# Expert result rows: copied by GpSimd and stored from GpSimd's queue in place of ScalarE's

## The chip, the cores and the metric
One core of one Trainium2 chip runs the whole program. The metric is the device time of one execution in microseconds, as the median of several runs. The five engines are TensorE (PE), VectorE (DVE), ScalarE (ACT), GpSimd (POOL) and SyncE (SP).

## What is computed
One hybrid block (dilated attention beside gated linear attention), a mixture of 32 experts with 4 chosen for each of 512 tokens, and a second block (pooling and an RWKV-style recurrence). The change lies in the mixture of experts:

```python
def expert_block(args):
    idx, e = args
    xb = xpad[idx]
    gu = xb @ w_gate_up[e] + b_gate_up[e]
    x_glu = jnp.minimum(gu[:, ::2], SWIGLU_LIMIT)
    x_lin = jnp.clip(gu[:, 1::2], -SWIGLU_LIMIT, SWIGLU_LIMIT)
    act = x_glu * jax.nn.sigmoid(SWIGLU_ALPHA * x_glu) * (x_lin + 1.0)
    return act @ w_down[e] + b_down[e]

out_buf = lax.map(expert_block, (tok_buf.reshape(n_blocks, MOE_BLOCK), blk_e))
out = jnp.zeros((T + 1, D), out_buf.dtype).at[tok_buf].add(out_buf)
```

The model's width is 1024, the experts' inner width 1024, all numbers are float32. `b_down` and the gates are applied in the stage after the experts.

## The kernel before
The program runs in stages. In `stage_experts` the tokens of each expert are cut into units of 32 rows; a unit's 32 x 1024 rows lie on 128 partitions as four quarters of 256 columns. The number of units is known only at run time (each engine loads it into a register, `units_on`), and each engine runs a loop over them, `Fori(1, units)`. The engines meet only through semaphores.

*SyncE* loads the weights, 32 experts of 12 chunks of 1 MB (8 of gate and up, 4 of down), into 18 slots of `staging`. A chunk's slot is free when the last unit of the expert that lay there has used it (`free`), and at most five loads are under way (L1657 issues, L1641 counts the arrival of the chunk four before).

*VectorE and ScalarE* copy three quarters of each chunk from `staging` to one of four places of `ring` (L1865, L1788): positions 0, 1, 3, 4, 6, 8, 9, 11 of a unit by VectorE, 2, 5, 7, 10 by ScalarE. The first quarter is read from `staging` directly.

*TensorE* does in each turn of its loop: `up(i)`, eight chunks of four column groups (L1730); `down(i - 1)`, four chunks (L1753), into bank 4; `turn_hidden(i)` (L1739); `turn_rows(i + 2)` (L1707); the bias of the next unit (L1717). `down` starts only once `y_read` says that bank 4 was read.

*ScalarE*'s turn: the fills of positions 5, 7 and 10, `gate`, `rows_turned`, the fill of position 2 of the next unit, then `read_y(i - 1)` (L1811), which copies the result of the unit before from bank 4 to `y_rows`, `store_y(i - 1)` (L1816), which issues its store to `expert_rows` in HBM, and `hidden_turned(i)` (L1799), which `down(i)` needs. `read_y` waits for `y_out`: the store before must have landed, as there is one `y_rows`.

```python
def read_y(n, done):
    act.wait_ge(chunk_done, done)
    act.wait_ge(y_out, 16 * n + 16)
    act.activation(y[:], k.bank(4)[:, 0:GLU], ACT.Copy).then_inc(y_read, 1)

def store_y(n):
    act.wait_ge(y_read, n + 1)
    act.sem_inc(y_seen, 1)
    act.dma_start(store_of(n * SLOTS), y[:]).then_inc(y_out, 16)
```

*GpSimd*'s turn: `move_rows(i + 2)` (L1681) waits for the gather of those rows and for `turn_rows` of the unit before them, and copies `rows_landing` to `rows`; `gather(i + 3)` loads the unit's code, copies its indices to `slot` (L1670) and issues the indirect DMA of its rows (L1673).

Of the kernel before, what the change touches and what calls it, by code (L numbers as in the profile page):

```python
# [21 lines left out]
P = 128  # L22
S = 512
NT = S // P
D = 1024
# [7 lines left out]
NE, TOPK = 32, 4  # L33
SLOTS = 32
QUARTERS = 4
EXTRA = (S * TOPK) // (SLOTS + 1)
NBLK = NE + EXTRA
# [4 lines left out]
TABLE = ENDS + NE + LINE  # L42
# [1493 lines left out]
def stage_experts(k):  # L1536

    nc, d = k.nc, k.d
    with ExitStack() as ctx:
        sb = lambda n, s, dt=F32: k.sb(n, s, dt, at=ctx)  # L1540
        sem = k.stage_semaphores(ctx)
# [6 lines left out]
        landing = sb("rows_landing", [P, D // QUARTERS])  # L1548
# [3 lines left out]
        glu = sb("glu", [P, GLU])  # L1552
        hT = sb("hiddenT", [P, 2, P])
        y = sb("y_rows", [P, D // QUARTERS])
        gsum = sb("gsum", [P, LINE])
        raw_bias = ring[:, RING - 1, 0:PART]
        hidden = glu
# [10 lines left out]
        rows_in = sem("rows_in")  # L1568
# [13 lines left out]
        turned_ps = sem("hidden_turned_ps")  # L1582
        hT_ready = sem("hiddenT_ready")
        y_read = sem("expert_y_read")
        y_seen = sem("expert_y_seen")
        y_out = sem("expert_y_out")
        settled = sem("early_settled")
# [3 lines left out]
        def units_on(eng):  # L1591
            return eng.value_load(k.table[0:1, TABLE - 1:TABLE], min_val=NE, max_val=NBLK)

        def expert_on(eng, i):
            return eng.value_load(k.table[0:1, bass.ds(i, 1)], min_val=0, max_val=NE - 1)

        def after(eng, sem, n):

            if not isinstance(n, int) or n > 0:
                eng.wait_ge(sem, n)  # L1600
# [21 lines left out]
        def store_of(n):  # L1622
            return d["expert_rows"][bass.ds(n, SLOTS), :].rearrange("r (c n) -> c r n", c=QUARTERS)

        with nc.Block() as block:
# [37 lines left out]
            @block.gpsimd  # L1663
            def _(pool):
                units = units_on(pool)
                by_quarter = d["h2"].rearrange("t (c n) -> (t c) n", c=QUARTERS)

                def gather(i, out, at, done):
                    code = pool.value_load(k.table[0:1, bass.ds(i + P, 1)], min_val=0, max_val=CODES - 1)
                    pool.tensor_copy(slot[:, at:at + 1], k.slots[:, bass.ds(code, 1)]).then_inc(slot_ready, 1)  # L1670
                    pool.wait_ge(slot_ready, i + 1)
                    pool.sem_inc(slot_seen, 1)
                    pool.indirect_dma_start(  # L1673
                        out=out[:], out_offset=None, in_=by_quarter,
                        in_offset=bass.IndirectOffsetOnAxis(ap=slot[:, at:at + 1], axis=0)).then_inc(done, 16)

                def move_rows(i):
                    pool.wait_ge(rows_in, 16 * i - 16)
                    pool.wait_ge(rows_ps, i)
                    pool.sem_inc(rows_free, 1)  # L1680
                    pool.tensor_copy(rows[:], landing[:]).then_inc(rows_here, 1)  # L1681
                    pool.wait_ge(rows_here, i + 1)
                    pool.sem_inc(rows_moved, 1)

                gather(0, y, 1, first_in[0])
                gather(1, rows, 2, first_in[1])
                gather(2, landing, 0, rows_in)
                for m in range(2):
                    pool.wait_ge(first_in[m], 16)
                    pool.sem_inc(rows_here, 1)  # L1690
                move_rows(2)
                gather(3, landing, 0, rows_in)
                with pool.Fori(1, units) as i:
                    move_rows(i + 2)
                    gather(i + 3, landing, 0, rows_in)
                pool.wait_ge(rows_in, 16 * units + 16)

            @block.tensor
            def _(pe):
# [82 lines left out]
            def _(act):  # L1782
                units = units_on(act)

                def fill(i, e, pos):
                    act.wait_ge(chunk_in, e * CHUNKS + (pos + 1))
                    after(act, chunk_done, i * CHUNKS + (pos - RING + 1))
                    act.activation(ring[:, pos % RING, :], staged(i, e, pos, PART, CHUNK - PART), ACT.Copy  # L1788
                                   ).then_inc(act_filled, 1)

                def gate(i):
                    act.wait_ge(lin_ready, i + 1)
                    after(act, turned_ps, i)
                    act.activation(glu[:], k.bank(0)[:, 0:GLU], ACT.Silu, scale=ALPHA).then_inc(glu_ready, 1)

                def hidden_turned(i):
                    act.wait_ge(turned_ps, i + 1)
                    act.wait_ge(chunk_done, i * CHUNKS + CHUNKS)
                    act.activation(hT[:].rearrange("p b n -> p (b n)"), k.bank(2)[:, 0:2 * P], ACT.Copy,  # L1799
                                   scale=1.0 / ALPHA).then_inc(hT_ready, 1)  # L1800

                def rows_turned(i, done):
                    act.wait_ge(rows_ps, i + 1)
                    after(act, chunk_done, done)
                    act.activation(rowsT[:].rearrange("p b n -> p (b n)"), k.bank(6)[:, 0:2 * P], ACT.Copy
                                   ).then_inc(rowsT_ready, 1)

                def read_y(n, done):
                    act.wait_ge(chunk_done, done)
                    act.wait_ge(y_out, 16 * n + 16)  # L1810
                    act.activation(y[:], k.bank(4)[:, 0:GLU], ACT.Copy).then_inc(y_read, 1)  # L1811

                def store_y(n):
                    act.wait_ge(y_read, n + 1)
                    act.sem_inc(y_seen, 1)
                    act.dma_start(store_of(n * SLOTS), y[:]).then_inc(y_out, 16)  # L1816

                act.sem_inc(y_out, 16)
                rows_turned(0, 0)
                fill(0, 0, 2)  # L1820
                act.wait_ge(bias_set, 1)
# [13 lines left out]
                with act.Fori(1, units) as i:  # L1835
                    e = expert_on(act, i)
                    fill(i, e, 5)
                    fill(i, e, 7)
                    fill(i, expert_on(act, i - 1), 10)
                    gate(i)  # L1840
                    rows_turned(i + 1, i * CHUNKS + KT)
                    fill(i + 1, expert_on(act, i + 1), 2)
                    read_y(i - 1, i * CHUNKS + CHUNKS)
                    store_y(i - 1)
                    hidden_turned(i)
                act.wait_ge(act_filled, units * len(BY_ACT) + 1)
                act.sem_inc(act_filled, 2)
# [2 lines left out]
                act.activation(k.gates[:], k.gates[:], ACT.Exp).then_inc(gate_exp, 1)  # L1850
                end = act.value_load(k.table[0:1, TABLE - 2:TABLE - 1], min_val=NE - 1, max_val=NBLK - 1)
                read_y(end, units * CHUNKS + CHUNKS)
                store_y(end)
                act.wait_ge(y_out, 16 * units + 16)
                act.sem_inc(y_seen, 1)

            @block.vector
            def _(dve):
# [1273 lines left out]
```

## Time and profile before

| | |
|---|---|
| median of 3 runs | 1996.08 us (1993.56 to 2001.99) |
| the profiled execution | 1999.55 us |
| its span, first to last instruction | 1997.8 us |
| TensorE's granted clock, mean | 0.929 |
| busy: PE / DVE / ACT / POOL | 85% / 57% / 43% / 16% |
| moved by DMA | 516.46 MB, mean 259 GB/s |
| weights of the experts' stage | 250 + 128 loads of 1 MB by SyncE, 6 early ones |
| stores of result rows | 80 of 128 KB on ScalarE's queue (q10) |
| gathers of rows | 83 of 128 KB on GpSimd's queue (q0) |

How to read it: busy shares are means over stages with different limits, and a matmul's group counts time in which others run beside it. What bounds a stage is read from the waits in that stretch. "Landing" is the time at which a DMA's completion was counted.

### The profile page before, as it was taken

Reading aid. Unit: us, or ns where it says so; the run is one execution under the profiler, and the core shown is the slowest. Engines: PE = TensorE matmul, PEld = TensorE weight load, DVE = VectorE, ACT = ScalarE, POOL = GpSimd, SP = SyncE. Lnnn points to the kernel's source line nnn. Section 1 sums busy time; section 2 is a strip of 40 time slices with the busy share of each in tenths; the row PEclk is TensorE's granted clock in tenths of the full one; section 3 lists DMA queues with packets and bytes.
Section 4 is the critical chain, followed back from the end, with each engine's and each line's share of the span. In section 5 each row is a group of like instructions: output and inputs, shape, how many; then the busy total and the mean of one; then the engine's idle time right before and its main releaser. Section 6 shows DMA issues by size and latency. Waiting matters only on the chain. (4 is left out here: it accounts for less than half of the span.)

```text
span 1997.8 us, 50227 instructions
## 1 busy us (share of the span) xinstructions
PE 1695.5 (85%) x16925; PEld 877.7 (44%) x16926; DVE 1139.1 (57%) x1698; ACT 859.4 (43%) x1131; POOL 326.4 (16%) x307
## 2 busy tenths in 40 slices
PE   6999888698898899888887789878887658998797
PEld 3999645232233333333332233333232226777763
DVE  5874535574566566555654456556554454784555
ACT  5334522254455455444543445445443334433411
POOL 0000000121222222222221122222111030260000
PEclk9999988798999999999998899999888778999999
DMA  8870850539669888992699986996898872221011
GB/s 315 281 264 11 230 206 35 239 151 425 264 273 423 366 338 338 425 401 105 260 424 404 400 336 278 424 374 279 346 426 331 341 260 69 79 74 45 6 53 42
DMA packets 134386, 516.46 MB, mean 259 GB/s; under 512 B 11411, under 2 KB 60324, under 8 KB 85029
## 3 DMA queue, kind: packets, MB, share of 16 engines
q1 hardware_dynamic: 116884, 483.61, 61.4%
q0 software_dynamic: 6720, 20.85, 2.8%
q10 hardware_dynamic: 10706, 10.96, 1.7%
q8 instruction: 51, 0.84, 0.2%
q14 instruction: 25, 0.20, 0.0%
HBM read 492.57 MB, written 22.81 MB: 258 GB/s over the span
## 5 line engine op out<-in xcount | busy, mean ns | idle before, releaser
L1865 DVE COPY ring<-staging 128x1536 f32 (+1 forms) x638 | 602.9, 961 | 428.9 <-PE banks L1730 285.7
L1730 PE MATMUL banks<-staging,rowsT 128*32 (+1 forms) x1268 | 650.1, 654 | 185.0 <-ACT ring L1788 149.8
L1730 PE MATMUL banks<-ring,rowsT 128*32 128x512 f32 x3840 | 661.1, 656 | 0.0
L1788 ACT ACTIVATE ring<-staging 128x1536 f32 (+1 forms) x319 | 465.3, 1481 | 400.3 <-PE banks L1730 145.4
L1730 PEld LDWEIGHTS banks<-staging,rowsT 128*32 128x32 f32 x1268 | 128.8, 115 | 630.3 <-issue 625.4
L1753 PE MATMUL banks<-staging,hiddenT 128*32 x1280 | 297.6, 387 | 2.3 <-ACT hiddenT L1799 2.1
L1753 PE MATMUL banks<-ring,hiddenT 128*32 128x256 f32 x3840 | 298.5, 386 | 0.0
L1753 PEld LDWEIGHTS banks<-staging,hiddenT 128*32 128x32 f32 x1280 | 141.9, 113 | 163.5 <-issue 71.2
L1681 POOL COPY rows<-rows_landing 128x256 f32<-128x256 f32 x80 | 74.8, 935 | 794.9 <-PE banks L1707 794.9
L1753 PEld LDWEIGHTS banks<-ring,hiddenT 128*32 128x32 f32 x3840 | 156.9, 113 | 0.0
L602 PE MATMUL banks<-w_in_hi,hT 128*128 128x256 f32 (+1 forms) x768 | 147.0, 291 | 1.1 <-issue 1.1
L1730 PEld LDWEIGHTS banks<-ring,rowsT 128*32 128x32 f32 x3840 | 144.9, 115 | 0.0
L1673 POOL DMA_INDIRECT rows_landing<-h_rows,slot x81 | 133.4, 1647 | 64.3 <-POOL slot L1670 64.3
L2208 PE MATMUL banks<-h3T,w_in_hi 128*128 128x512 f32 x400 | 128.9, 404 | 1.4 <-DVE h3T L2386 1.4
L602 PEld LDWEIGHTS banks<-w_in_hi,hT 128*128 128x128 f32 x768 | 122.2, 193 | 3.1 <-issue 3.0
L602 PE MATMUL banks<-w_in_lo,hT 128*128 128x256 f32 (+1 forms) x384 | 109.5, 285 | 0.0
L1670 POOL COPY slot<-slots 128x1 int32 x83 | 49.4, 595 | 276.0 <-issue 206.2
L1874 DVE TENSOR_SCALAR lin<-banks 128x256 f32<-128x256 f32 x80 | 34.0, 425 | 96.3 <-PE banks L1730 96.3
L2208 PEld LDWEIGHTS banks<-h3T,w_in_hi 128*128 128x128 f32 x400 | 75.6, 190 | 22.9 <-issue 4.1
L1799 ACT ACTIVATE hiddenT<-banks 128x256 f32<-128x256 f32 x80 | 30.7, 384 | 113.0 <-PE banks L1730 98.7
L2208 PE MATMUL banks<-h3T,w_in_lo 128*128 128x512 f32 x200 | 78.5, 392 | 0.0
L1811 ACT ACTIVATE y_rows<-banks 128x256 f32<-128x256 f32 x80 | 30.0, 375 | 108.3 <-DMA expert_rows<-y_rows 97.5
(435 smaller groups left out, 1949.7 us busy)
## 6 DMA issues: line engine op xcount, KB each, us to landing
staging<-in_w_gate_up SPq DMA_DIRECT2D x250, 1024.0 KB, 13.3
staging<-in_w_down SPq DMA_DIRECT2D x128, 1024.0 KB, 13.3
stage<-in_w_mod SPq DMA_DIRECT2D x21, 1024.0 KB, 5.4
stage<-in_w_in SPq DMA_DIRECT2D x25, 512.0 KB, 4.0
stage<-in_w_in SPq DMA_DIRECT2D x11, 1024.0 KB, 6.7
expert_rows<-y_rows ACTq DMA_DIRECT2D x80, 128.0 KB
expert_rows<-catT SPq DMA_DIRECT2D x1, 7936.0 KB
early<-in_w_gate_up SPq DMA_DIRECT2D x6, 1024.0 KB, 13.5
```

The lines of the kernel that those rows point to most:

```text
L602: mm = pe.matmul(k.bank(4 + t)[:, 0:w], hT[:, a, q, tt], b[:, q, :], start=(q == 0 and a == 0 and b is hi), stop=(q == KT - 1 and a == 1))
L1670: pool.tensor_copy(slot[:, at:at + 1], k.slots[:, bass.ds(code, 1)]).then_inc(slot_ready, 1)
L1673: pool.indirect_dma_start(out=out[:], out_offset=None, in_=by_quarter, in_offset=bass.IndirectOffsetOnAxis(ap=slot[:, at:at + 1], axis=0)) ...
L1681: pool.tensor_copy(rows[:], landing[:]).then_inc(rows_here, 1)
L1730: mm = pe.matmul(k.bank(0)[c * SLOTS:(c + 1) * SLOTS, :], rowsT[:, q % 2, row], w, start=first and q == 0, stop=not first and q == KT - 1, ...
L1753: mm = pe.matmul(k.bank(4)[c * SLOTS:(c + 1) * SLOTS, 0:GLU], hT[:, b, m * SLOTS:(m + 1) * SLOTS], w, start=(m == 0 and b == 0), stop=(m = ...
L1788: act.activation(ring[:, pos % RING, :], staged(i, e, pos, PART, CHUNK - PART), ACT.Copy).then_inc(act_filled, 1)
L1799: act.activation(hT[:].rearrange("p b n -> p (b n)"), k.bank(2)[:, 0:2 * P], ACT.Copy, scale=1.0 / ALPHA).then_inc(hT_ready, 1)
L1811: act.activation(y[:], k.bank(4)[:, 0:GLU], ACT.Copy).then_inc(y_read, 1)
L1865: dve.tensor_copy(ring[:, pos % RING, :], staged(i, e, pos, PART, CHUNK - PART)).then_inc(dve_filled, 1)
L1874: dve.tensor_scalar(lin[:], k.bank(0)[:, GLU:PART], LIMIT + 1.0, 1.0 - LIMIT, ALU.min, ALU.max).then_inc(lin_ready, 1)
L2208: mm = pe.matmul(k.bank(n % 4), w[:, n % NW, q, :], hT[:, b, q, :], start=(q == 0 and a == 0), stop=(q == KT - 1 and a == 2))
```

## The change
A new buffer `rows_leaving` takes the place of `y_rows` as the source of the store. GpSimd copies `y_rows` to it, waits for its own copy, and issues the store from its own queue, at the end of each turn of its loop; the turn of unit 1 now stands ahead of the loop. ScalarE's `read_y` waits for `y_free` (GpSimd has copied the rows before) in place of `y_out` (they have landed), and issues no store. GpSimd's copy waits for `y_read`, and for `y_out` of the store before.

```diff
+        leaving = sb("rows_leaving", [P, D // QUARTERS])
...
+                def store_rows(n):
+                    pool.wait_ge(y_read, n + 1)
+                    after(pool, y_out, 16 * n)
+                    pool.sem_inc(y_due, 1)
+                    pool.tensor_copy(leaving[:], y[:]).then_inc(y_free, 1)
+                    pool.wait_ge(y_free, n + 2)
+                    pool.sem_inc(y_seen, 1)
+                    pool.dma_start(store_of(n * SLOTS), leaving[:]).then_inc(y_out, 16)
...
-                with pool.Fori(1, units) as i:
+                pool.sem_inc(y_free, 1)
+                move_rows(3)
+                gather(4, landing, 0, rows_in)
+                store_rows(0)
+                with pool.Fori(2, units) as i:
                     move_rows(i + 2)
                     gather(i + 3, landing, 0, rows_in)
+                    store_rows(i - 1)
+                end = pool.value_load(k.table[0:1, TABLE - 2:TABLE - 1], min_val=NE - 1, max_val=NBLK - 1)
+                store_rows(end)
                 pool.wait_ge(rows_in, 16 * units + 16)
+                pool.wait_ge(y_out, 16 * units)
+                pool.sem_inc(y_seen, 1)
...
                 def read_y(n, done):
                     act.wait_ge(chunk_done, done)
-                    act.wait_ge(y_out, 16 * n + 16)
+                    act.wait_ge(y_free, n + 1)
                     act.activation(y[:], k.bank(4)[:, 0:GLU], ACT.Copy).then_inc(y_read, 1)
 
-                def store_y(n):
-                    act.wait_ge(y_read, n + 1)
-                    act.sem_inc(y_seen, 1)
-                    act.dma_start(store_of(n * SLOTS), y[:]).then_inc(y_out, 16)
-
-                act.sem_inc(y_out, 16)
...
                     read_y(i - 1, i * CHUNKS + CHUNKS)
-                    store_y(i - 1)
                     hidden_turned(i)
...
                 read_y(end, units * CHUNKS + CHUNKS)
-                store_y(end)
-                act.wait_ge(y_out, 16 * units + 16)
-                act.sem_inc(y_seen, 1)
```

On ScalarE, at the end of its turn of the experts' loop, the order before is this:

```order
L1788 ACTIVATE ring<-staging 128x1536
L1809 REGISTER_ALU
L1810 ISA
L1811 ACTIVATE y_rows<-banks 128x256
L1816 ISA
L1816 DMA expert_rows<-y_rows 4x32x256
L1799 ACTIVATE hiddenT<-banks 128x256
```

and after the change this:

```order
L1809 ACTIVATE ring<-staging 128x1536
L1830 REGISTER_ALU
L1832 ACTIVATE y_rows<-banks 128x256
L1820 ACTIVATE hiddenT<-banks 128x256
L1850 REGISTER_ALU
L1850 COMPARE_AND_BRANCH
```

The store is gone from between the copy of the result rows and `hiddenT`.

On GpSimd, the whole turn of its loop before:

```order
L1681 COPY rows<-rows_landing 128x256
L1682 REGISTER_ALU
L1669 ISA
L1669 TENSOR_LOAD table
L1669 ISA x2
L1670 ISA
L1670 COPY slot<-slots 128x1
L1671 REGISTER_ALU
L1673 DMA rows_landing<-h_rows,slot 128x256
L1693 REGISTER_ALU
L1693 COMPARE_AND_BRANCH
```

and the second half of the turn after the change:

```order
L1673 COPY slot<-slots 128x1
L1674 REGISTER_ALU
L1676 DMA rows_landing<-h_rows,slot 128x256
L1603 ISA
L1692 COPY rows_leaving<-y_rows 128x256
L1693 REGISTER_ALU
L1695 ISA
L1695 DMA expert_rows<-rows_leaving 4x32x256
L1709 REGISTER_ALU
L1709 COMPARE_AND_BRANCH
```

The copy to `rows_leaving` and the store stand behind the gather, and ahead of the next turn's move of rows. TensorE's, VectorE's and SyncE's instructions keep their order.

## Rows read from the trace of the kernel before

**Rows 1.** Timeline of TensorE, turning the hidden rows: start us, us, instruction.
```profile
897.99 0.44 PE L1739 MATMUL banks<-sq,glu 128*128 128x128 f32 x2
...
911.64 0.44 PE L1739 MATMUL banks<-sq,glu 128*128 128x128 f32 x2
...
929.36 0.44 PE L1739 MATMUL banks<-sq,glu 128*128 128x128 f32 x2
...
941.26 0.44 PE L1739 MATMUL banks<-sq,glu 128*128 128x128 f32 x2
```

**Rows 2.** The tile `y_rows`: its durations min/median/max in ns, first and last start.
```profile
L1811 ACT ACTIVATE y_rows<-banks x80: 360/383/390, 409.9 to 1596.3; 128x256 f32<-128x256 f32 x80
```

**Rows 3.** TensorE's waits from 410 to 1600: total us, times, longest us.
```profile
PE banks L1730 <- ACT ring L1788: 149.8, 92, 4.7
```

**Rows 4.** ScalarE's waits, the same stretch.
```profile
ACT y_rows L1811 <- DMA expert_rows<-y_rows: 97.5, 36, 4.5
```

**Rows 5.** Timeline of ScalarE, two units in a loaded stretch; idle time in brackets.
```profile
900.60 0.39 ACT L1811 ACTIVATE y_rows<-banks 128x256 f32<-128x256 f32 x1 [1.63 <-DMA expert_rows<-y_rows]
901.25 1.07 ACTq L1816 DMA_DIRECT2D expert_rows<-y_rows  x1
...
916.62 0.38 ACT L1811 ACTIVATE y_rows<-banks 128x256 f32<-128x256 f32 x1 [4.01 <-DMA expert_rows<-y_rows]
...
918.43 0.38 ACT L1799 ACTIVATE hiddenT<-banks 128x256 f32<-128x256 f32 x1 [1.42 <-issue]
919.87 2.86 ACT L1788 ACTIVATE ring<-staging 128x1536 f32 x2 [1.06 <-issue]
```

**Rows 6.** Timeline of ScalarE where the DMA engines have little to do.
```profile
942.77 1.05 ACTq L1816 DMA_DIRECT2D expert_rows<-y_rows  x1
...
954.06 0.36 ACT L1811 ACTIVATE y_rows<-banks 128x256 f32<-128x256 f32 x1
```

**Rows 7.** DMA queues from 654 to 669: packets, MB, share of 16 engines.
```profile
q1 hardware_dynamic: 845, 6.14, 96.8%
q10 hardware_dynamic: 132, 0.13, 2.5%
q0 software_dynamic: 48, 0.13, 2.2%
```

**Rows 8.** Timeline of GpSimd, one turn.
```profile
912.47 1.11 POOL L1681 COPY rows<-rows_landing 128x256 f32<-128x256 f32 x1 [8.59 <-PE banks L1707]
...
915.80 1.72 POOL L1673 DMA_INDIRECT rows_landing<-h_rows,slot  x1 [0.79 <-POOL slot L1670]
```

**Rows 9.** Lines L1673, L1681 and L1865: durations min/median/max in ns; a landing.
```profile
L1673 POOL DMA_INDIRECT rows_landing<-h_rows,slot x81: 966/1722/1726, 375.0 to 1559.7; - x81
...
DMA to landing us min/median/max: 6.2/6.2/6.2
...
L1681 POOL COPY rows<-rows_landing x80: 397/1091/1152, 384.9 to 1557.5; 128x256 f32<-128x256 f32 x80
...
L1865 DVE COPY ring<-staging x638: 945/960/1187, 386.9 to 1591.2; 128x1536 f32 x158, 128x1536 f32<-128x1536 f32 x2
```

**Rows 10.** Windows: length, PE, PEld, DVE, ACT, POOL busy, PEclk, DMA share, GB/s.
```profile
457.00:515.00 58.00, 44.42 (x405) 13.76 (x402) 26.88 (x35) 21.65 (x25) 7.54 (x9) 0.82 1.01 425
636.00:667.00 31.00, 25.49 (x277) 9.88 (x270) 17.28 (x23) 14.65 (x17) 6.77 (x6) 0.94 1.01 426
929.00:989.00 60.00, 59.05 (x679) 23.42 (x672) 42.34 (x56) 35.61 (x41) 16.92 (x15) 1.00 0.40 155
```

**Rows 11.** ScalarE's waits for the store from 636:698, 819:912, 1007:1055 and 1256:1350.
```profile
ACT y_rows L1811 <- DMA expert_rows<-y_rows: 10.7, 4, 4.1
...
ACT y_rows L1811 <- DMA expert_rows<-y_rows: 14.8, 6, 3.7
...
ACT y_rows L1811 <- DMA expert_rows<-y_rows: 7.6, 3, 3.6
...
ACT y_rows L1811 <- DMA expert_rows<-y_rows: 13.0, 5, 3.7
```

**Rows 12.** Timeline behind the last unit.
```profile
1601.83 0.94 POOL L2323 DMA_INDIRECT mixer<-expert_rows,dest  x1 [41.13 <-POOLq L192]
```

More of the change, by code:

```diff
@@ L1584, in stage_experts @@
         y_read = sem("expert_y_read")
+        y_due = sem("expert_y_due")
+        y_free = sem("expert_y_free")
         y_seen = sem("expert_y_seen")
```

## The prediction, made before the changed kernel ran

> **What bounds the kernel now.** I read the views in this order: the waits of each engine in the expert stage, the timeline of single units, the windows with the DMA share, and the queues. A unit is one pass of 32 rows through one expert; there are 80 of them. The reference's routing, worked out on its inputs, gives the 32 experts these units in order: 5, 1, 2, 5, 3, 2, 2, 3, 3, 3, 2, 2, 2, 7, 2, 2, 1, 2, 2, 3, 4, 2, 2, 2, 3, 4, 1, 2, 3, 1, 1, 1.
>
> The reader should first see what a unit costs when nothing holds it up. TensorE turns the hidden rows once a unit, and two such rows are 941.26 - 929.36 = 11.9 us apart [rows 1]. At that pace 80 units are 952 us. ScalarE's 80 copies of the result rows start from 409.9 to 1596.3 us [rows 2], 79 steps in 1186 us, where 79 x 11.9 would be 940: about 246 us are lost. TensorE's idle time there ends mostly on ScalarE's fills of the ring: 149.8 us in 92 waits [rows 3]. Why is ScalarE late? It waited 97.5 us, in 36 of the 80 units, for the store of the last result rows to land before it could overwrite `y_rows` [rows 4].
>
> The timeline shows how that reaches TensorE. The store issued at 901.25 lets the next copy start only at 916.62, so the round trip is 15.4 us; the copy stood 4.01 us, then came the issue, then `hiddenT` at 918.43, and only at 919.87 the fills that TensorE needs [rows 5]. The two units from 897.99 to 929.36 take 13.65 and 17.72 us, 31.4 in place of 23.8 [rows 1]. That is 7.6 us lost for 1.63 + 4.01 = 5.6 us of waiting: each microsecond of this wait costs TensorE about 1.35. Where the DMA engines have little to do, the wait isn't there: the store issued at 942.77 is no hindrance at 954.06 [rows 6].
>
> Why 15 us for 128 KB? In 15 us of a loaded stretch ScalarE's queue q10 moved 132 packets for 0.13 MB: 128 rows of 1 KB and four small ones, so I read it as four engines with 32 rows each. The weights' queue q1 had 845 packets and 96.8% of 16 engines, about 0.27 us a packet (0.968 x 16 x 15 / 845) [rows 7]. If an engine takes one packet from each queue in turn, 32 rows wait behind 32 weight packets, some 10 us, and issue and completion make up the rest.
>
> **The change, part by part.**
> *Removed on ScalarE: the wait for the landing.* Upper bound of what it gives: 97.5 x 1.35 = 132 us. *Removed on ScalarE: the issue.* From the start of the copy to `hiddenT` are now 1.8 us, about 1.4 of them after the copy has ended [rows 5]. In a unit without the wait TensorE doesn't wait for ScalarE at all (11.9 us), so this gives nothing more there; in the others it lies in the 1.35. I cost it at 0; the cover is TensorE's own work.
>
> *Added on GpSimd: copy, wait, issue.* Its unit today runs from 912.47 to 917.52, 5.1 us, of which the copy of rows is 1.11 and the wait between the slot's copy and the gather 0.79 [rows 8]. The new copy has the same shape (128x256 f32): 1.1 us. A wait on its own copy: 0.8. The issue: the gather's takes 0.97 to 1.73 us [rows 9]; I take 1.7. Together 3.6, so that GpSimd is occupied 8.7, with the loop's registers about 9 us of 11.9. Queued behind the new wait for `y_read` are the next move of rows and the next gather: both start about 4 us later in their unit than now. The moved rows are needed one unit later, 11.9 us after the point at which the move may start, and are ready after about 4 + 1.1; cover 6 us. The gather is issued about 9 us into the unit and lands 6.2 us after its issue [rows 9], while the next move begins at 11.9 + 4; that just fits, with a cover of under 1 us ahead of the 6 us of the rows themselves. Cost: 0. If the cover went, `turn_rows` on TensorE would wait.
>
> *The new round trip.* ScalarE now waits for GpSimd's copy of the rows before, and that copy for the landing of the store before it. GpSimd's queue q0 moved a gather of the same 128 KB as 48 packets, 32 of 4 KB and 16 small ones [rows 7]: two data packets an engine in place of 32 rows. If the store is cut like this, its round trip is the 6.2 us of the gather, plus copy 1.1 and wait 0.8: a period of 8.1 us, under 11.9. The bounds, since no row shows a store on this queue: 6.2 at the low end, and at the high end today's 32 rows an engine, 15.4 with 0.65 us more for the issue. I take the low one, because both transfers have rows of 1 KB on both sides. The Trainium skill ("DMA: Bandwidth & Descriptors", "Queues, rings and completion order") says that the slowest dimension of the access pattern picks how many engines share a transfer, for both kinds of queue. The four engines of q10 agree with that, as the store's pattern is 4x32x256. By it the new store would also sit on four engines; with 4 KB packets that is 8 an engine, about 6 x 0.45 us more, a period of 10.8 us, still under 11.9, and the sum stays.
>
> The copy and the issue could also be slowed by VectorE. GpSimd's copies take 397 ns to 1152 ns, nearly always the long value, while VectorE's 638 fills stay between 945 and 1187 [rows 9]: GpSimd is the one that gives way, and 1.1 and 1.7 already contain it. VectorE: 0. The Trainium skill ("SBUF — State Buffer", "SBUF: two separate sides") has a rule against this change: while VectorE copies f32 within SBUF, GpSimd can't write the descriptors of its DMAs, and an issue of 620 ns takes about 3100. The trace agrees in direction, not in size: 1.73 is the longest gather. With 3.1 for each of its two DMAs GpSimd would be occupied 11.8 us a unit, just at the pace, and nothing would be left to spare.
>
> *What the weights take back.* In the two units 636 to 667 the DMA share is 1.01 at 426 GB/s [rows 10]: an expert's 12.6 MB with the rows of two units can't come in less than 30.8 us, and two units want 23.8. So a two-unit expert gains only as far as weights are there ahead: 18 slots less 12 are half an expert, 15.4 us at most. The waits in the two-unit runs are 10.7 + 14.8 + 7.6 + 13.0 = 46.1 of the 97.5 us [rows 11]. Lower end: no lead, all of that comes back as waits for weights, and 51.4 x 1.35 = 69 us are saved. Upper end: full lead; then only the two runs of three such experts overdraw it, by 3 x 7.0 - 15.4 = 5.6 each, and 132 - 11 = 121 are saved. The one lone and one two-unit expert from 457 to 515 should need 60.9 us of stream and took 58, so that hardly 3 us of lead was there, although five units stood before them [rows 10]. But the experts of three units and more leave 4.9 us and more each for the stream to get ahead, and from 929 to 989, in the expert of seven, its share is 0.40: there it had run out of free slots. Between the two I take the middle, 95.
>
> *The four engines relieved.* The store's packets are 2.5% of 16 engines over 15 us, 6.0 us of work, 1.5 on each of four [rows 7]. If weight loads waited for these, up to 1.2 us a loaded unit would come free. A share of 1.01 over all sixteen says that the others weren't idle meanwhile; I take 0 and let it widen the low end.
>
> *The end.* The last copy starts at 1596.3 and the gathers of the next stage at 1601.83 [rows 12]; the copy and the wait on GpSimd put 1 us to 2 us in. Cost 1.
>
> Sum: 1999.55 - 95 + 1 = 1905.6 for the profiled execution, which stands 3.5 us above the median of the runs. **Forecast 1902 us.**
>
> **The rivals.**
> *A. The weights take back more.* Each two-unit expert stays at 30.8 us. For it: share 1.01, and 457 to 515. Against it: 929 to 989 has a share of 0.40 [rows 10], so after long experts all slots must be full. Time: 1996 - 69 + 1 = 1928; with some of the other units' gain lost as well, up to 1960.
> *B. Slower: the store's round trip on GpSimd's queue becomes the pace.* If GpSimd sends the rows one by one on four engines, the trip is 16.0 us, and copy and wait make the period 17.9, against 16.0 between the copies at 900.60 and 916.62. It decides from 11.9 us on (gain shrinks) and makes the kernel slower above 16. In the 36 units that wait today that is 36 x 1.9 = 68 us: 2064. Against it: the 48 packets of the gather.
> *C. Nothing changes.* The fills come late for TensorE's own reasons (ScalarE's fills wait for TensorE too) and the stage is held by the weights throughout. Against it: 929 to 989, and the timeline. Or GpSimd's period comes out near 15. Time 1996, from 1986 to 2006.
>
> **How the numbers follow.** A measurement of this kernel can tell about 0.5%, 10 us, from no change. The forecast's own case, 1876 to 1928, has 0.64; A 0.20, B 0.10, C 0.06. Faster 0.84, same 0.06, slower 0.10. The range leaves out B and C, and takes in A to 1960; below, 1865, for the four engines. That leaves out 0.16 and the tails.
>
> **What would show it.** The wait of `y_rows` for the DMA must be gone from ScalarE's waits, and nothing of size for GpSimd in its place. TensorE's waits for ScalarE's fills fall from 149.8 us to about half, and those for VectorE's fills, 32 us now, rise, as waiting for weights shows there. The DMA share in 800 to 1500 rises. Units in the loaded stretches come at 11.9 us, with single long ones behind two-unit runs. q0 has 48 packets more a unit. GpSimd's idle time before the copy of rows, now nearly all of its time, stays above 2 us a unit. Wrong would be: ScalarE's copy waits for GpSimd's, GpSimd's copy for a DMA of over 10 us, or `turn_rows` on TensorE for `rows`.

## The result and the profile after

The changed kernel takes 1901.84 us (median of 4 runs, 1900.64 to 1903.0) against 1998.28 us (4 runs): a ratio of 0.952, 95% interval 0.9495 to 0.9542. The forecast was 1902. The profiled execution took 1903.0 us with a span of 1901.4, 96.4 less than before. The total is right to the microsecond; the terms it was summed from are not, as the rest shows, so that this closeness is luck.

| from the traces, us | before | after | difference |
|---|---|---|---|
| first to last copy of result rows, 79 steps | 1186.4 | 1083.2 | -103.2 |
| TensorE's wait into the next stage | 5.8 | 10.8 | +5.0 |
| all else in the span | 805.6 | 807.4 | +1.8 |
| span | 1997.8 | 1901.4 | -96.4 |

**Waits.** ScalarE's waits of the changed kernel from 410 to 1600 (total us, times, longest) have one line on the result rows, in place of [rows 4]:

```profile
ACT y_rows L1832 <- PE banks L1774: 1.0, 1, 1.0
```

The 97.5 us are gone. They haven't moved to GpSimd: of its waits up to 1495 the largest is for new result rows, and the landing of a store held it up four times.

```profile
POOL rows_leaving L1692 <- ACT y_rows L1832: 606.5, 76, 24.4
...
POOL rows_leaving L1692 <- DMA expert_rows<-rows_leaving: 16.7, 4, 5.3
```

TensorE's waits, against [rows 3]:

```profile
PE banks L1751 <- ACT ring L1809: 67.4, 40, 3.1
PE banks L1751 <- DVE ring L1876: 42.2, 39, 4.4
...
PE banks L2169 <- DVE z L2456: 10.8, 1, 10.8
```

Those for ScalarE's fills fell from 149.8 to 67.4 us, those for VectorE's rose from 32.2 to 42.2: what is left comes mostly with the arrival of weights. The last line is the wait into the next stage.

**The unit.** Here is ScalarE's timeline of one unit, at the place that [rows 5] and [rows 6] show of before:

```profile
902.93 0.36 ACT L1832 ACTIVATE y_rows<-banks 128x256 f32<-128x256 f32 x1
903.19 0.38 ACT L1820 ACTIVATE hiddenT<-banks 128x256 f32<-128x256 f32 x1
905.31 1.49 ACT L1809 ACTIVATE ring<-staging 128x1536 f32 x1 [1.74 <-PE banks L1751]
...
914.44 0.36 ACT L1832 ACTIVATE y_rows<-banks 128x256 f32<-128x256 f32 x1
```

A unit now takes 914.44 - 902.93 = 11.5 us, where [rows 1] had 11.9 as the pace of an undisturbed one. 53 of the 79 steps run at 11.5, where 20 ran at 11.9 before. That was not forecast. The granted clock is 1.00 at both places, so it isn't the clock. `hiddenT` follows the copy by 0.26 us in place of 1.8, and the fills wait for TensorE instead of the other way round.

**GpSimd.** The first two rows below are the tiles' durations (min/median/max in ns), the others its timeline of one turn.

```profile
L1692 POOL COPY rows_leaving<-y_rows x80: 393/410/1107, 409.6 to 1494.2; 128x256 f32<-128x256 f32 x80
...
L1695 POOL DMA_DIRECT2D expert_rows<-rows_leaving x80: 713/874/1542, 410.8 to 1495.3; - x80
...
607.32 0.42 POOL L1692 COPY rows_leaving<-y_rows 128x256 f32<-128x256 f32 x1 [5.18 <-ACT y_rows L1832]
608.53 0.87 POOL L1695 DMA_DIRECT2D expert_rows<-rows_leaving  x1 [0.78 <-POOL rows_leaving L1692]
609.39 0.41 POOL L1684 COPY rows<-rows_landing 128x256 f32<-128x256 f32 x1
...
611.72 1.12 POOL L1676 DMA_INDIRECT rows_landing<-h_rows,slot  x1 [0.81 <-POOL slot L1673]
```

The turn is 607.32 to 612.84, 5.5 us, where 8.7 were forecast. Both copies take 0.41 us in place of 1.1. They now start as a fill of VectorE ends or just before, and run mostly in the gaps in which VectorE waits for TensorE (607.50 to 608.17 and 609.49 to 609.89 here).

**The DMA engines.** The packets of the page, before and then after:

```profile
DMA packets 134386, 516.46 MB, mean 259 GB/s; under 512 B 11411, under 2 KB 60324, under 8 KB 85029
```
```profile
DMA packets 135347, 516.60 MB, mean 272 GB/s; under 512 B 20051, under 2 KB 58724, under 8 KB 85989
...
q0 software_dynamic: 18240, 31.46, 4.6%
```

q0 had 6720 packets before, so each of the 80 stores is 11520 / 80 = 144 packets. The small ones rose by 8640 = 80 x 108; with the four that ScalarE's store had, that is 112 a store, and 32 packets are left for its 128 KB, 4 KB each. The last store goes out alone, so the order of its packets can be read: these are all DMA packets first from 1496.0 to 1497.6, then from 1497.6 to 1500.0.

```profile
DMA packets 112, 0.02 MB, mean 11 GB/s; under 512 B 108, under 2 KB 108, under 8 KB 112
```
```profile
DMA packets 32, 0.11 MB, mean 48 GB/s; under 512 B 4, under 2 KB 4, under 8 KB 32
```

Of the 112 small packets 108 come first, with four of the 4 KB ones, and only four come with the other 28. By size the 112 are 96 of 16 bytes and 16 of 4 bytes, and 4 bytes is also the size of ScalarE's four small ones. I read the 16 as completions: twelve of engines that carry no data, and four of engines that carry all of it, eight packets of 4 KB each. So on GpSimd's queue too four engines carry the store; what differs from ScalarE's is that the rows go four to a packet. Over the stage (410 to 1596, and 410 to 1490) the DMA share rose:

```profile
410.00:1596.00 1186.00, 1001.64 (x10517) 372.87 (x10516) 663.43 (x869) 558.71 (x630) 250.50 (x234) 0.92 0.83 341
```
```profile
410.00:1490.00 1080.00, 968.09 (x10480) 371.50 (x10476) 666.05 (x862) 550.22 (x626) 261.33 (x392) 0.94 0.91 375
```

**The end of the stage.** GpSimd's timeline there, against [rows 12]:

```profile
1494.19 0.40 POOL L1692 COPY rows_leaving<-y_rows 128x256 f32<-128x256 f32 x1 [3.60 <-DMA expert_rows<-rows_leaving]
1495.35 0.71 POOL L1695 DMA_DIRECT2D expert_rows<-rows_leaving  x1 [0.76 <-POOL rows_leaving L1692]
1502.82 1.02 POOL L2334 DMA_INDIRECT mixer<-expert_rows,dest  x1 [6.76 <-POOLq L192]
```

From the last copy of ScalarE (1492.2) to the next stage's first gather it is 10.6 us, where it was 5.5 before: the last copy of GpSimd waits for the landing of the store before it, then come a wait, an issue and a landing.

### The profile page after: what moved, and what is told of

Read it like the earlier page. It is cut to its first block and busy times, and to the rows that moved or that the text cites. A ratio compares the mean times of both kernels' runs of the same rounds, so it can differ in the third digit from the quotient of the medians.

```text
span 1901.4 us, 50539 instructions
## 1 busy us (share of the span) xinstructions
PE 1665.0 (88%) x16925; PEld 878.1 (46%) x16926; DVE 1144.6 (60%) x1698; ACT 852.6 (45%) x1131; POOL 338.2 (18%) x467
## 5 line engine op out<-in xcount | busy, mean ns | idle before, releaser
L1809 ACT ACTIVATE ring<-staging 128x1536 f32 (+1 forms) x319 | 472.1, 1485 | 526.6 <-PE banks L1751 260.5
L1751 PE MATMUL banks<-staging,rowsT 128*32 (+1 forms) x1268 | 607.1, 622 | 112.7 <-ACT ring L1809 67.4
L1751 PE MATMUL banks<-ring,rowsT 128*32 128x512 f32 x3840 | 617.6, 624 | 0.0
L1774 PE MATMUL banks<-staging,hiddenT 128*32 x1280 | 308.4, 397 | 2.0 <-ACT hiddenT L1820 0.5
L1774 PE MATMUL banks<-ring,hiddenT 128*32 128x256 f32 x3840 | 309.5, 397 | 0.0
L1692 POOL COPY rows_leaving<-y_rows 128x256 f32<-128x256 f32 x80 | 34.5, 431 | 623.2 <-ACT y_rows L1832 606.5
L1676 POOL DMA_INDIRECT rows_landing<-h_rows,slot x81 | 108.8, 1343 | 65.9 <-POOL slot L1673 65.9
L1695 POOL DMA_DIRECT2D expert_rows<-rows_leaving x80 | 71.3, 891 | 66.7 <-POOL rows_leaving L1692 60.6
L602 PEld LDWEIGHTS banks<-w_in_lo,hT 128*128 128x128 f32 x384 | 74.2, 193 | 1.9 <-issue 1.9
L1673 POOL COPY slot<-slots 128x1 int32 x83 | 23.2, 279 | 285.8 <-issue 235.2
## 6 DMA issues: line engine op xcount, KB each, us to landing
staging<-in_w_gate_up SPq DMA_DIRECT2D x250, 1024.0 KB, 12.6
```

The lines of the kernel that those rows point to most:

```text
L602: mm = pe.matmul(k.bank(4 + t)[:, 0:w], hT[:, a, q, tt], b[:, q, :], start=(q == 0 and a == 0 and b is hi), stop=(q == KT - 1 and a == 1))
L1676: pool.indirect_dma_start(out=out[:], out_offset=None, in_=by_quarter, in_offset=bass.IndirectOffsetOnAxis(ap=slot[:, at:at + 1], axis=0)) ...
L1692: pool.tensor_copy(leaving[:], y[:]).then_inc(y_free, 1)
L1695: pool.dma_start(store_of(n * SLOTS), leaving[:]).then_inc(y_out, 16)
L1751: mm = pe.matmul(k.bank(0)[c * SLOTS:(c + 1) * SLOTS, :], rowsT[:, q % 2, row], w, start=first and q == 0, stop=not first and q == KT - 1, ...
L1774: mm = pe.matmul(k.bank(4)[c * SLOTS:(c + 1) * SLOTS, 0:GLU], hT[:, b, m * SLOTS:(m + 1) * SLOTS], w, start=(m == 0 and b == 0), stop=(m = ...
```

## The experiments

Three theories stood against each other. *The trip*: the old store's round trip of 15 us is the cause, and this comes from its access pattern. *The buffer*: `rows_leaving` decouples ScalarE from the landing. *The issue*: what counts is that ScalarE no longer issues. The kernel before ran again beside every group.

### e1: the copy stays, ScalarE issues the store

```diff
 def store_rows(n):
     ...
     pool.tensor_copy(leaving[:], y[:]).then_inc(y_free, 1)
-    pool.wait_ge(y_free, n + 2)
-    pool.sem_inc(y_seen, 1)
-    pool.dma_start(store_of(n * SLOTS), leaving[:]).then_inc(y_out, 16)
...
     hidden_turned(i)
+    act.wait_ge(y_free, n + 2)
+    act.sem_inc(y_seen, 1)
+    act.dma_start(store_of(n * SLOTS), leaving[:]).then_inc(y_out, 16)
```

> The changed kernel, but ScalarE issues the store of rows_leaving, behind hiddenT. Theory 1 (the trip of the store is what counted: ScalarE's queue puts 32 rows on each of four engines, issue to landing 14.3 us in a loaded stretch; on GpSimd's queue it is 7 to 7.7): GpSimd's copy must still wait for the landing, ScalarE for the copy, so the period stays at 15 to 16 us in loaded stretches and the time at 1980 to 2010 us, with 90 us or more of waits that begin with the DMA. Theory 2 (the second buffer decouples ScalarE from the landing): 1900 to 1920 us. Theory 3 (the issue on ScalarE is what counted): about half of the gain is gone, 1930 to 1960, and no wait for a DMA.

Measured: 2028.58 us, ratio 1.014 (1.0102 to 1.0175). It is slower than the kernel before, and by more than the theory of the trip had it. GpSimd's waits, and ScalarE's timeline around two stores:

```profile
POOL rows_leaving L1692 <- DMA expert_rows<-rows_leaving: 463.8, 41, 12.4
```
```profile
899.79 1.05 ACTq L1834 DMA_DIRECT2D expert_rows<-rows_leaving  x1
...
911.23 0.38 ACT L1817 ACTIVATE hiddenT<-banks 128x256 f32<-128x256 f32 x1
915.65 1.08 ACTq L1834 DMA_DIRECT2D expert_rows<-rows_leaving  x1
918.17 2.86 ACT L1806 ACTIVATE ring<-staging 128x1536 f32 x2 [6.57 <-issue]
```

Two issues are 15.9 us apart, as before the change. The buffer alone gives nothing: as long as one store at a time is in flight and takes 15 us, its pace is everyone's. ScalarE now waits for GpSimd's copy, which waits for the landing, and the fills stand behind that; even an undisturbed unit takes 12.5 us (27 of the 79 steps). The theory of the buffer falls, for one store in flight; two in flight were not tried.

### e2: GpSimd stores `y_rows` itself, no copy, no second buffer

```diff
 def store_rows(n):
+    pool.wait_ge(y_out, 16 * n)       # not for unit 0
+    pool.sem_inc(y_free, 1)
     pool.wait_ge(y_read, n + 1)
-    after(pool, y_out, 16 * n)
-    pool.sem_inc(y_due, 1)
-    pool.tensor_copy(leaving[:], y[:]).then_inc(y_free, 1)
-    pool.wait_ge(y_free, n + 2)
     pool.sem_inc(y_seen, 1)
-    pool.dma_start(store_of(n * SLOTS), leaving[:]).then_inc(y_out, 16)
+    pool.dma_start(store_of(n * SLOTS), y[:]).then_inc(y_out, 16)
```

> The changed kernel without rows_leaving and without the copy: GpSimd stores y_rows itself, and tells ScalarE of the landing once its own gather is issued. Theory 1: a trip of 7 to 8 us ends before the next result rows are due at 11.5 us, so the copy and the buffer weren't needed: 1895 to 1910 us, waits of y_rows under 15 us in sum. Theory 2: ScalarE again waits for a landing, so the old waits come back: 1970 us or more.

Measured: 1902.73 us, ratio 0.9515 (0.9487 to 0.9543), no different from the changed kernel. The tile `y_rows` (its store's issue in ns, and its time to landing in us):

```profile
L1693 POOL DMA_DIRECT2D expert_rows<-y_rows x80: 712/1546/1565, 409.1 to 1497.8; - x80
...
DMA to landing us min/median/max: 3.9/9.1/10.6
```

9.1 us, and at most 10.6, lie under the 11.5 of a unit. So the copy that the change adds isn't needed.

### e3: the old store with another slowest dimension

The store writes its 128 partitions to one contiguous stretch. The rows then stand in another order in HBM and the next stage gathers other values; the work is the same.

```diff
 def store_of(n):
-    return d["expert_rows"][bass.ds(n, SLOTS), :].rearrange("r (c n) -> c r n", c=QUARTERS)
+    return d["expert_rows"][bass.ds(n, SLOTS), :].rearrange("r (c n) -> (r c) n", c=QUARTERS)
```

> The kernel before, but the store writes the 128 partitions to one contiguous stretch of expert_rows, so that its slowest dimension is 128 and not 4; the same bytes in another order, so the rows that the next stage gathers hold other values. Buffer, wait and issue on ScalarE stay. Theory 1: the trip falls from 14.3 us to 6 to 9, ScalarE's wait for it from 97.5 us to under 15; units at full pace keep 11.9 us since ScalarE still issues: 1905 to 1935 us. Theories 2 and 3: nothing that counts was changed, 1985 to 2005 us.

Measured: 1889.58 us, ratio 0.9446 (0.9417 to 0.9474). With the buffer, the wait and the issuing engine of before, this one line gives more than the whole change. The tile `y_rows`, and the page's packets:

```profile
L1816 ACTq DMA_DIRECT2D expert_rows<-y_rows x80: 347/349/398, 410.5 to 1487.8; - x80
...
DMA to landing us min/median/max: 1.7/6.8/7.7
```
```profile
DMA packets 135346, 516.46 MB, mean 273 GB/s; under 512 B 12371, under 2 KB 61284, under 8 KB 85989
```

The store lands after 6.8 us in the median, and its issue takes 349 ns in place of 1072. There are 960 packets more than before, all of the small kind: 12 a store, so 16 in place of 4. That fits one completion for each engine that takes part, sixteen and four, and the theory of the trip. It went below the forecast of 1905 to 1935 because the pace fell to 11.5 too. The 12 us under the changed kernel are 5.9 in the 79 steps (1077.3) and 6.6 in TensorE's wait into the next stage, which is 4.2 here and 10.8 there.

### e4 and e7: what the issue costs

Why 11.5 and not 11.9? In e4 ScalarE also issues a small load in each turn:

```diff
     read_y(i - 1, i * CHUNKS + CHUNKS)
+    small_dma(i - 1)                  # d["token"], 128 partitions of 20 bytes
     hidden_turned(i)
```

> The changed kernel, plus one small load (128 partitions of 20 bytes) that ScalarE issues between the copy of the result rows and hiddenT, where the store's issue stood. It tests the pace of a unit alone: 11.9 us before, 11.5 after. If the issue on ScalarE makes its fill of position 5 late by 0.4 us in every unit: the pace is 11.9 again, TensorE shows a gap of about 0.4 us in the middle of the eight chunks, and the time rises by 8 to 28 us, to 1910 to 1930. If the pace has another cause (the four engines of the store, the longer turn of GpSimd): 11.5 stays, and 1900 to 1905 us.

Measured: 1906.31 us, ratio 0.9536 (0.9507 to 0.9565); the pace stayed at 11.5. The load's issue took 0.34 us and came ahead of the copy, where ScalarE has time, so that it answered only for a short issue. The time lies between the two forecasts, 4.5 us above the changed kernel, and no run shows why. In e7 the added DMA is a small store with the old pattern, behind a wait for the copy, and nobody waits for it to land:

```diff
+    act.wait_ge(y_read, n + 1)
+    act.sem_inc(small_due, 1)
+    act.dma_start(d["small"][bass.ds(n * SLOTS, SLOTS), :].rearrange("r (c n) -> c r n", c=QUARTERS),
+                  k.sq[:, ONES, 0:8]).then_inc(small_out, 16)
```

> The changed kernel, plus a store of 128 pieces of 32 bytes in the old pattern (4x32x8) that ScalarE issues between the result rows and hiddenT; nobody waits for its landing. The issue of this pattern takes 1.05 to 1.07 us, where the small load took 0.34 and the contiguous store 0.35. If this issue made the unit 11.9 us long in place of 11.5: pace 11.9, a gap of 0.4 us ahead of chunk 5, 1906 to 1925 us. If not, 11.5 and under 1906.

Measured: 1919.55 us, ratio 0.9588 (0.9561 to 0.9615), 17.7 above the changed kernel. Its ScalarE:

```profile
890.07 0.36 ACT L1834 ACTIVATE y_rows<-banks 128x256 f32<-128x256 f32 x1
890.69 1.08 ACTq L1839 DMA_DIRECT2D small_rows<-sq  x1
891.87 0.38 ACT L1822 ACTIVATE hiddenT<-banks 128x256 f32<-128x256 f32 x1 [1.44 <-PE banks L1753]
893.31 2.86 ACT L1811 ACTIVATE ring<-staging 128x1536 f32 x2 [1.05 <-PE banks L1753]
...
901.98 0.37 ACT L1834 ACTIVATE y_rows<-banks 128x256 f32<-128x256 f32 x1
```

The same intervals as before the change, and the pace is 11.9 again. The two fills of positions 5 and 7 stand back to back behind it, and the fill of position 5 is what TensorE misses by 0.4 us: its matmuls at 894.13 and 894.93 are 0.80 us apart, the others 0.43. So an issue of 1.07 us between the copy and `hiddenT` costs 0.4 us a unit even where no one waits for a landing.

### e5: two buffers, and the last store from ScalarE

```diff
-    pool.tensor_copy(leaving[:], y[:]).then_inc(y_free, 1)
-    pool.wait_ge(y_free, n + 2)
-    pool.sem_inc(y_seen, 1)
-    pool.dma_start(store_of(n * SLOTS), leaving[:]).then_inc(y_out, 16)
+    pool.sem_inc(y_free, 1)
+    pool.dma_start(store_of(n * SLOTS), y_of(n)).then_inc(y_out, 16)   # half n % 2 of y_rows
...
     read_y(end, units * CHUNKS + CHUNKS)
+    act.wait_ge(y_read, end + 1)
+    act.sem_inc(y_last_due, 1)
+    act.dma_start(store_of(end * SLOTS), y_of(end)).then_inc(y_last, 16)
```

> The changed kernel without the copy: ScalarE writes to two halves of y_rows in turn, GpSimd stores each straight from there, one store in flight, and the last unit's store is issued by ScalarE itself without waiting for the one before. It tests the end of the stage, where the changed kernel lost 5 us (TensorE's wait for the next stage is 10.8 us long, 5.8 before), since the last copy waits 3.6 us for a landing and is followed by a wait and a slower landing. If these are the cause, 4 to 6 us come back: 1896 to 1898 us. If the loss comes from the next stage's own work: 1901 to 1903.

Measured: 1900.38 us, ratio 0.9494 (0.9468 to 0.952). TensorE's wait into the next stage:

```profile
PE banks L2177 <- DVE z L2464: 6.2, 1, 6.2
```

The wait is down from 10.8 to 6.2, so the 5 us at the end do come from the last store. But the time fell by 1.5 only: the 79 steps took 1087.3 us against 1083.2. Why these 4 us were lost is open; GpSimd's issue has a median of 1247 ns there, against 874. (e2, also without the copy, has 1546 ns and 1088.6 us.)

### e6 and e11: a complete result on sixteen engines

e6 is the kernel before with four stores of 32 partitions a unit, all from ScalarE:

```diff
-    act.dma_start(store_of(n * SLOTS), y[:]).then_inc(y_out, 16)
+    for c in range(QUARTERS):
+        act.dma_start(d["expert_rows"][bass.ds(n * SLOTS, SLOTS), c * GLU:(c + 1) * GLU],
+                      y[c * SLOTS:(c + 1) * SLOTS, :]).then_inc(y_out, 16)
```

> The kernel before, but each unit's rows go out as four stores of 32 partitions each from ScalarE, so that the slowest dimension is 32 and sixteen engines share each; the result is complete and in order, the buffer and the wait for the landing are those of before. Theory 1 (the four engines are the whole cause): four issues of 0.35 us in place of one of 1.07, a landing after 7 to 9 us, no wait for it, 1888 to 1905 us. If the queue rather than the pattern were the cause: 1990 us or more.

Measured: 1926.2 us, ratio 0.962 (0.9593 to 0.9648). The wait for the landing is gone, as the theory of the trip wants, but the forecast was missed by 21 us: the four issues take 1.77 us together, and all stands at 12.4 us a unit.

```profile
904.24 0.36 ACT L1811 ACTIVATE y_rows<-banks 128x256 f32<-128x256 f32 x1
904.85 1.77 ACTq L1817 DMA_DIRECT2D expert_rows<-y_rows  x4
906.71 0.38 ACT L1799 ACTIVATE hiddenT<-banks 128x256 f32<-128x256 f32 x1 [2.12 <-PE banks L1730]
```

e11 issues the same four stores one turn later, behind the fill of position 7:

```diff
     fill(i, e, 7)
+    store_y(i - 2)                    # from turn 2 on; turn 1 stands ahead of the loop
     ...
     read_y(i - 1, i * CHUNKS + CHUNKS)
-    store_y(i - 1)
     hidden_turned(i)
```

> The kernel before, with four stores of 32 partitions each, issued by ScalarE not between the result rows and hiddenT but one turn later, behind its fill of position 7. If the 12.4 us a unit of the run with four stores (issues of 1.77 us ahead of the next fill) is the late fill of position 5: the pace is 11.5 to 11.6 again, and the time 1886 to 1900 us, as with the contiguous store. The landing must come within about 8 us of the issue, else ScalarE waits for it and the pace stays at 12 or more, 1915 to 1930.

Measured: 1894.66 us, ratio 0.9488 (0.9464 to 0.9513), and 1081.5 us for the 79 steps. There is no single pace: 21 steps lie between 11.3 and 11.8 us, 39 others between 10.6 and 13.5. The waits for the landing have become short, but they are there in 43 units; the line below is from 400 to 1490:

```profile
ACT y_rows L1811 <- DMA expert_rows<-y_rows: 25.7, 43, 1.5
```

Of the kernels with a complete result this has the lowest median, 7 us under the changed one (1893.08 to 1900.7 against 1900.64 to 1903.0, measured in different groups; the intervals of the two ratios overlap, so that the order isn't settled), without GpSimd and without a second buffer.

### e8, e9, e10: what holds the stage now

In e8 half of each weight chunk is left out from the 37th on:

```diff
+    whole = CHUNK if m < 2 * STAGED else CHUNK // 2
     sp.dma_start(staging[:, m % STAGED * CHUNK:m % STAGED * CHUNK + whole],
                  (up(e, c) if c < KT else down(e, c - KT))[:, 0:whole])
```

> The changed kernel with only half of each weight chunk loaded from the 37th chunk on (the other half of each slot keeps old values, so the results are others). It prices what the stream of weights still costs: with it out of the way the 79 steps should take 79 x 11.5 = 909 us and a little for the first units, in place of 1083, so 1730 to 1750 us. If another limit lay close behind (GpSimd's turn, the gather), the pace would be above 11.5 and the time over 1780.

Measured: 1753.57 us, 4 us above the forecast's end; the 79 steps take 938 us. 69 of 79 steps run at 11.5 us, and TensorE's waits from 410 to 1345 are down to these:

```profile
PE banks L1752 <- ACT ring L1810: 12.8, 15, 1.9
PE banks L1752 <- DVE ring L1877: 9.7, 11, 2.6
```

So the weights' stream still costs the changed kernel about 148 us (the lower clock that comes with its waits, 0.939 against 0.968 in the mean, is in that), and the new turn of GpSimd isn't a limit close behind: the pace stays at 11.5. e9 and e10 allow two more loads under way, in the changed kernel and in e5:

```diff
-AHEAD = 4
+AHEAD = 6
```

> The changed kernel with up to seven weight loads under way in place of five (AHEAD 6 in place of 4). What is left of lost time in its stage (1083 us for 79 steps, 909 at full pace) is the wait for weights. If the stream loses time when it starts up behind a lull, more loads under way give 5 to 15 us: 1887 to 1897. If it is at its rate wherever it is needed: 1898 to 1904. If the store, which shares the engines, now lands later than 11 us, GpSimd's waits for it grow and the time with them, to 1910 or more.

> The run with two buffers and no copy (1900.4 us), with up to seven weight loads under way. The same as for the run before, less the 4 us at the stage's end: 1885 to 1896 if the start-up of the stream counts, 1897 to 1902 if not.

Measured: 1903.24 us (ratio 0.9522, 0.9503 to 0.9541) and 1898.88 us (0.9509, 0.9488 to 0.9531). Neither differs from its base. In e9 a load's median time to landing rose from 12.6 to 16.2 us, and nothing else moved; the stream is at its rate where it is needed.

## Why the prediction was right, point by point

*The bound.* The reading was right: the trip of the store, ScalarE's wait, the late fills. That the 15 us come from 32 rows on each of four engines, each behind a weight packet, was inferred from 132 packets [rows 7]. e3 shows the pattern to be the cause: 6.8 us without it, by the same engine and queue. For the waiting behind weight packets the trace of before has a comparison: q10 from 905.0 to 916.5, beside the weights, and from 943.5 to 946.0, where nothing else is under way.

```profile
q10 hardware_dynamic: 132, 0.13, 3.2%
```
```profile
q10 hardware_dynamic: 132, 0.13, 17.5%
```

The packets' own time is 3.2% of 16 x 11.5 and 17.5% of 16 x 2.5, so 5.9 and 7.0 engine-us: beside the weights they are no slower, they only stand further apart. The 128 rows begin over 10.8 us there and over 1.7 here, which is one row an engine in 0.34 us, about one weight packet and one row. That fits engines which take one packet from each queue in turn; no run tests it apart.

*The wait removed, 132 us less what the weights take back, together 95.* **This term was too large.** e7 has the wait removed and an issue of the old length kept: its 79 steps take 1106.9 us against 1186.4, so the wait gives 79.5 us. The two ends, 69 and 121, held it, but the middle was not the place: it was nearer to rival A, in which the two-unit experts give all of it back. The changed kernel shows why in its stretch from 457 to 515, as one of [rows 10]:

```profile
457.00:515.00 58.00, 44.20 (x406) 14.16 (x410) 27.44 (x36) 22.85 (x27) 9.46 (x15) 0.82 1.01 425
```

Share 1.01, 425 GB/s, the same as before: where the stream is saturated nothing is to be had. The upper end of 121 also counted only the two runs of three two-unit experts as overdrawing the lead, and passed over the experts of one unit. The run 2, 2, 1, 2, 2 behind the expert of seven took 151.2 us before (ScalarE's copies at 977.88 and 1129.08) and takes 142.7 now (925.95 and 1068.63); at 11.5 us its nine units would be 104.

*The issue on ScalarE, costed at 0.* **This step failed.** "TensorE doesn't wait for ScalarE at all" in a unit without the wait was read from the pace of 11.9 us as if it were TensorE's own. It is 11.5, and the trace of before had it. These are TensorE's waits from 929 to 989, the stretch that [rows 10] shows as undisturbed, and its timeline at chunk 5 of one unit:

```profile
PE banks L1730 <- ACT ring L1788: 0.9, 5, 0.2
```
```profile
946.21 0.59 PE L1730 MATMUL banks<-staging,rowsT 128*32 x1
...
947.01 0.61 PE L1730 MATMUL banks<-staging,rowsT 128*32 x1 [0.19 <-ACT ring L1788]
```

TensorE does wait for ScalarE, once in each of the five units; the view gives 0.19 us each, while the two starts are 0.80 us apart in place of 0.43. The window's 59.05 us of busy time in 60 say the same; the changed kernel has 50.00 in the 50 us from 900 to 950. The waits are 0.9 of the 149.8 us of [rows 3], small enough to be read as nothing. e7 against the changed kernel: 1106.9 - 1083.2 = 23.7 us in the stage, 17.7 us in the medians. Some 20 of them are 0.4 us in each of about 50 units; the 6 us between the two numbers come back behind ScalarE's last copy, from where the program takes 402.3 us in e7 and 409.2 in the changed kernel.

*The end, costed at 1.* It was 5.0 us. The part forgotten is the 3.60 us in which the last copy waits for the landing of the store before, and the longer way to landing.

*Sum.* Within the stage 79.5 + 23.7 = 103.2 in place of 95, less 5.0 in place of 1, and 1.8 elsewhere: 96.4 against 94. Over the whole profiled executions the two steps are 1999.55 - 1920.47 = 79.1 and 1920.47 - 1903.0 = 17.5 us. The errors of the terms cancel, and nothing in the prediction made them do so.

*GpSimd's turn, 9 us, and its cover.* It is 5.5 us; the cover held with room. I had taken its copies at the 1.1 us that they had beside VectorE's fills, and the new store delays them into a gap: 0.41. The rule of the Trainium skill ("SBUF — State Buffer", "SBUF: two separate sides"), that a DMA from GpSimd of some 620 ns takes some 3100 beside VectorE's copies, has no support in size here: the store's issue took 713 to 1542 ns, and VectorE's fills, which last only 960 ns each, kept that. (The prediction took the page's figures, which are of a DMA, for its issue.) In direction it holds: e2 issues the store right behind ScalarE's copy and takes 1546 in the median against 874.

*The trip on GpSimd's queue, 6.2 us by the gather.* **This step failed too, without a cost.** The store isn't cut as the gather is: q0 got 144 packets a unit and not 48, and the packets of the last store show four engines with eight of 4 KB each. The landing can't be read in the changed kernel. In e9, the same kernel with more loads under way, it is 8.5 us in the median and 9.8 at most; in e2, with an issue 0.7 us longer, 9.1. The prediction's other case, four engines with 4 KB packets, had 6.2 + 2.7 = 8.9 us. All this lies under the 11.5 of a unit, so that the sum was spared. The rule that the pattern's slowest dimension picks the engines (the Trainium skill, "DMA: Bandwidth & Descriptors", "Why a DMA increments its semaphore by 16 and not by 1") fits both queues here: with the slowest dimension 4 there are four small packets a store from ScalarE and four last completions from GpSimd, with 128 sixteen from ScalarE. Its page also names an exception for some direct copies from GpSimd, which get all sixteen; this store isn't one of them.

*Rival B*, slower through a trip that sets the pace, did not come about on GpSimd's queue: its four engines were there, its 32 packets of one row each were not. e1 is that mechanism on ScalarE's: one store in flight, 15.9 us apart, and 1.4% slower than before.

## What to carry to other kernels

Look at a store's access pattern before moving it to another engine or giving it a buffer: beside the stream of weights a slowest dimension of 4 cost 8 us to landing, and 0.7 us more to issue. One line took both away, with the rows left in an order that the next stage would have to be taught; in the right order it took four issues, at a place where ScalarE has time for them. GpSimd's queue helped with the same four engines; I put that down to its packets of 4 KB, which no run changes by themselves. A second buffer doesn't help against a transfer that takes longer than a turn as long as only one may be in flight. And a pace that is the same in every undisturbed turn isn't yet the engine's own: look for a short wait that comes once in every turn, and compare with the busy time, before costing a removed step at nothing.

## What was unexpected of the hardware

- The issue of a DMA on ScalarE took 1047 to 1175 ns with the pattern 4x32x256, 1053 to 1185 with 4x32x8, 347 to 398 with 128x256, and 322 in the median with 32x256. It goes with the pattern, not with the bytes.
- The same 4x32x256 store went out as 132 packets from ScalarE (128 of 1 KB) and 144 from GpSimd (32 of 4 KB, the others small) and I read both as sitting on four engines.
- GpSimd's copy of 128x256 took 0.41 us alone and 1.1 beside VectorE's copies, while these didn't grow.
- Under the saturated stream two more loads under way changed their time to landing, 12.6 to 16.2 us, and not the time.
